# Order and budgets in a fused expert stage: where comparisons, gathers and reloads stand

## The reference

```python
q = (hb @ wq).reshape(tc, PEER_HEADS, 2, PEER_HALF)
s = jnp.einsum('thpk,hpnk->thpn', q, keys)                  # 8 heads, 2 halves, 128 keys
s_top, i_top = lax.top_k(s, PEER_TOPK)                      # 16 each
cand = s_top[:, :, 0, :, None] + s_top[:, :, 1, None, :]
cid = i_top[:, :, 0, :, None] * N_KEYS + i_top[:, :, 1, None, :]
best, pos = lax.top_k(cand.reshape(tc, PEER_HEADS, -1), PEER_TOPK)
eid = jnp.take_along_axis(cid.reshape(tc, PEER_HEADS, -1), pos, -1)
g = jax.nn.softmax(best.astype(jnp.float32), -1).astype(hb.dtype)
act = jax.nn.gelu(jnp.einsum('td,thed->the', hb, u[eid]), approximate=False)
return jnp.einsum('the,thed->td', g * act, v[eid])
```

## Time and profile before

| | us |
|---|---|
| median of 3 runs | 3791.73 (3785.59 to 3792.56) |
| the profiled execution | 3789.86 |
| its span | 3787.8 |
| granted TensorE clock over the span | 0.974 |
| busy: TensorE, weight loads, VectorE, ScalarE, GpSimd | 3556.8, 3153.1, 2732.2, 1689.3, 395.3 |
| phase U without tables, from 488.2 | 177.7 |
| phase U with tables, from 666.0 | 542.8 |
| between the phases | 23.5 |
| phase V | 558.6 |
| from V's last product to the next one | 34.0 |

### The profile page before, as it was taken

The page is one execution under the profiler, slowest core; times in us unless marked ns, Lnnn a source line. Parts: engine busy times, 40 slices in busy tenths (PEclk is TensorE's granted clock), DMA queues, the critical chain, the costliest instruction groups (busy, mean ns, idle before and its releaser), DMA issues. The chain is left out here.

```text
span 3787.8 us, 56067 instructions
## 1 busy us (share of the span) xinstructions
PE 3556.8 (94%) x21807; PEld 3153.1 (83%) x21807; DVE 2732.2 (72%) x5456; ACT 1689.3 (45%) x3029; POOL 395.3 (10%) x282
## 2 busy tenths in 40 slices
PE   7999999999997999998699999999997899989899
PEld 5777998999897877887577999998886888988798
DVE  4557366878786888888546797778887767766775
ACT  4344233555554333333434444443334535564554
POOL 0000000000454343343200000000000000000000
PEclk9999999999999999999899999999998999999999
DMA  5133366544899999998213575556665213442243
GB/s 229 63 132 133 114 244 253 186 168 167 324 352 346 332 390 365 369 381 310 85 51 145 184 231 186 167 184 229 251 242 187 112 72 146 181 169 90 83 173 139
DMA packets 181767, 773.02 MB, mean 204 GB/s; under 512 B 22976, under 2 KB 70592, under 8 KB 131584
## 3 DMA queue, kind: packets, MB, share of 16 engines
q1 hardware_dynamic: 144640, 635.20, 46.3%
q0 software_dynamic: 36864, 134.23, 9.4%
HBM read 699.38 MB, written 69.99 MB: 203 GB/s over the span
## 5 line engine op out<-in xcount | busy, mean ns | idle before, releaser
L2907 DVE TENSOR_TENSOR expert_ring_low<-expert_ring,expert_high 128x1024 fp32r<-128x1024 f32 x256 | 312.9, 1222 | 169.9 <-ACT expert_high L3236 166.6
L2192 ACT ACTIVATE expert_high<-expert_ring 128x1024 fp32r<-128x1024 f32 x256 | 270.6, 1057 | 211.3 <-PE ps L2119 211.3
L1922 DVE TENSOR_TENSOR expert_ring_low<-expert_ring,expert_high 128x1024 fp32r<-128x1024 f32 x256 | 311.7, 1219 | 70.7 <-ACT expert_high L2192 70.7
L3133 PE MATMUL ps<-hidden_high,expert_high 128*128 128x384 f32 x1024 | 353.7, 345 | 0.0
L3135 PE MATMUL ps<-hidden_high,expert_ring_low 128*128 128x384 f32 x1024 | 344.2, 336 | 0.0
L3134 PE MATMUL ps<-hidden_low,expert_high 128*128 128x384 f32 x1024 | 343.8, 336 | 0.0
L3236 ACT ACTIVATE expert_high<-expert_ring 128x1024 fp32r<-128x1024 f32 x256 | 270.0, 1055 | 118.0 <-PE ps L3170 112.5
L3424 POOL DMA_INDIRECT x<-in_peer_rows,spots x128 | 181.4, 1417 | 1107.7 <-DVE spots L2979 605.0
L2088 PE MATMUL ps<-peer_hT_high_peer,expert_high 128*128 128x256 f32 x1024 | 293.9, 287 | 0.6 <-DVE expert_ring_low L1922 0.5
L2090 PE MATMUL ps<-peer_hT_high_peer,expert_ring_low 128*128 128x256 f32 x1024 | 287.0, 280 | 0.0
L2089 PE MATMUL ps<-peer_hT_low,expert_high 128*128 128x256 f32 x1024 | 287.0, 280 | 0.0
(11 more groups left out here) (777 smaller groups left out, 9762.4 us busy)
## 6 DMA issues: line engine op xcount, KB each, us to landing
expert_ring<-in_peer_u SPq DMA_DIRECT2D x128, 1024.0 KB
expert_ring<-in_peer_v SPq DMA_DIRECT2D x128, 1024.0 KB
weight_ring<-in_ffn_w_up SPq DMA_DIRECT2D x22, 2048.0 KB, 7.5
weight_ring<-in_w_in SPq DMA_DIRECT2D x14, 2048.0 KB, 7.3
weight_ring<-in_w_mod SPq DMA_DIRECT2D x12, 2048.0 KB, 7.5
mod_slot<-in_w_mod SPq DMA_DIRECT2D x12, 2048.0 KB, 10.5
pair_weights<-pair_weights_out SPq DMA_DIRECT2D x24, 1024.0 KB
gelu_first<-gelu_out SPq DMA_DIRECT2D x62, 384.0 KB
```

The costliest lines, as they stand in the source:

```text
L1922: dve.tensor_tensor(piece(low, n), piece(raw, n), high[:, n % LEAD, :].bitcast(F32), ALU.subtract).then_inc(low_done, 1)
L2192: act.activation(high[:, n % LEAD, :], piece(raw, n), ACT.Identity).then_inc(high_done, 1)
L2907: dve.tensor_tensor(self.piece(G.e_low, n), self.piece(G.e_raw, n), G.e_high[:, n % LEAD, :].bitcast(F32), ALU.subtract).then_inc(self.S.l ...
L3133: pe.matmul(o, b[:, s], B.hs[0][:, c, 0:DW], start=(c == 0), stop=False)
```

## The change

VectorE's and ScalarE's order within a round of phase U: compares, and shares, come first. In 12 rounds (60 to 82, every second) two groups are built, so the last group stands in round 115. The budgets are new: 3900 ns in the first rounds, 3300 with tables, 2200 once the selection is done, none from round 120 on, 1450 in phase V. The last 20 gelu rows stay on the chip (16 in a new buffer, `gelu_kept`). SyncE issues the first loads of gelu rows and pair weights when round 125 has been scored; the pair weights' buffer moves to the place of the table's stage, one-hot and share buffers. The first V round takes its tiles in the order 1, 2, 0, so only the third waits for the last gelu. `x` is reloaded at round 124 of phase V.

```diff
-EARLY_NS, TABLE_NS, DOWN_NS = 2600, 2300, 1700
+EARLY_NS, TABLE_NS, PICKS_NS, DOWN_NS = 3900, 3300, 2200, 1450
+PAUSE_FROM = 120
+STAY, RING = 20, 4
+    def gelu_at(self, e):
+        return self.B.ge_out[:, e % RING, :] if e < N_KEYS - STAY + RING else self.B.ge_kept[:, e - (N_KEYS - STAY + RING), :]
+    def tables_in(self, r):
+        return [g for g in range(TABLES) if TABLE_ROUND[g] == r]
+DOUBLED = range(60, 84, 2)
+TABLE_ROUND = [r for r in range(TABLES_AT, N_KEYS) for _ in range(2 if r in DOUBLED else 1)][0:TABLES]
...
+    def up_budget(self, r):
+        if "selected" not in self.at:
+            return EARLY_NS if r < TABLES_AT - 1 else TABLE_NS
+        return PICKS_NS if r < PAUSE_FROM else 0
@@ ExpertsVector.run, phase U
+            for g in self.tables_in(r + 1):
+                self.equal(dve, g)
             if r < N_KEYS - 1:
                 self.split_low(dve, r + LEAD)
-            if 0 <= r + 1 - TABLES_AT < TABLES:
-                self.equal(dve, r + 1 - TABLES_AT)
-            left += EARLY_NS if r < TABLES_AT - 1 else TABLE_NS
+            left += self.up_budget(r)
             while left > 0:
                 left -= next(pieces, left)
@@ ExpertsTensor.products_v
-        for t in range(DT):
+        for t in (1, 2, 0):
+            if r == 0 and t == 0:
+                pe.wait_ge(S.gelu_done, N_KEYS)
@@ ExpertsScalar.run, phase U
+            if r == N_KEYS - 1:
+                self.high_weights(act, 0)
+                self.high_weights(act, 1)
+            for g in self.tables_in(r + 1):
+                self.shares(act, g)
             self.gelu(act, r)
             if r in (0, 2):
                 keep_rows(r // 2)
             self.split_high(act, r + LEAD)
-            if 0 <= r + 1 - TABLES_AT < TABLES:
-                self.shares(act, r + 1 - TABLES_AT)
...
-            if r > TABLES_AT:
-                self.table_out(act, r - TABLES_AT - 1)
+            for g in self.tables_in(r - 1):
+                self.table_out(act, g)
@@ ExpertsSync.run
+            if p == UNITS_U - 2:
+                assert stored == BLOCKS
+                sp.wait_ge(S.table_ready, DT)
+                for b in range(2):
+                    sp.wait_ge(self.ge_stored[b], 16 * (N_KEYS - STAY) // (2 * UJ))
+                self.load_ge(sp, 0)
+                self.load_ge(sp, 1)
+                for b in range(2):
+                    sp.wait_ge(self.w_stored[b], 16 * BLOCKS // 2)
+                self.load_w(sp, 0)
+                self.load_w(sp, 1)
...
             if r == N_KEYS - E_SLOTS:
+                sp.wait_ge(S.aw_done, self.weights_end(W_LOADS - 2))
+                sp.dma_start(B.x_last[:, :], G.x_spill[:, SPARSE, :]).then_inc(S.x_landed, 16)
+                sp.wait_ge(S.dotted, PAIRS)
+                sp.dma_start(G.x[:, 0:SPARSE, :], G.x_spill[:, 0:SPARSE, :]).then_inc(S.x_landed, 16)
                 G.ws.refill(sp, S.pv_done, (N_KEYS - E_SLOTS,))
         G.ws.refill(sp, S.pv_done, (N_KEYS, N_KEYS, N_KEYS))
-        sp.wait_ge(S.dotted, PAIRS)
-        sp.dma_start(G.x[:, 0:SPARSE, :], G.x_spill[:, 0:SPARSE, :]).then_inc(S.x_landed, 16)
@@ first_experts
-    B.w_in = room(96, 24).take("pair_weights_in", [P, 2, BLOCKS, 8 * BLOCK], F32)
+    B.w_in = room(16, 24).take("pair_weights_in", [P, 2, BLOCKS, 8 * BLOCK], F32)
+    B.ge_kept = room(96, 24).take("gelu_kept", [P, STAY - RING, DW], F32)
```

More of the change, by code:

```diff
@@ L2876, in expert @@
     def expert(self, r):
-        return (r + N_KEYS - KEPT) % N_KEYS
+        return (r + N_KEYS - STAY) % N_KEYS
+    def gelu_at(self, e):
+        return self.B.ge_out[:, e % RING, :] if e < N_KEYS - STAY + RING else self.B.ge_kept[:, e - (N_KEYS - STAY + RING), :]
     def scores_of(self, g):
@@ L3046, in weigh @@
         n, j = self.weights_of(r)
-        m = r // 4 - 1
-        if r < KEPT:
+        m = (r - STAY) // 4
+        if r < STAY:
             dve.wait_ge(S.gelu_done, self.expert(r) + 1)
@@ L3055, in weigh @@
             dve.wait_ge(S.aw_split, r)
-        ge = B.ge_out[:, r, :] if r < KEPT else B.ge_in[:, m % 2, r % 4, :]
+        ge = self.gelu_at(self.expert(r)) if r < STAY else B.ge_in[:, m % 2, r % 4, :]
         w = B.w_in[:, n % 2, :, j * BLOCK:(j + 1) * BLOCK]
@@ L3079, in run @@
             at["now"] = r
+            for g in self.tables_in(r + 1):
+                self.equal(dve, g)
             if r < N_KEYS - 1:
                 self.split_low(dve, r + LEAD)
-            if 0 <= r + 1 - TABLES_AT < TABLES:
-                self.equal(dve, r + 1 - TABLES_AT)
-            left += EARLY_NS if r < TABLES_AT - 1 else TABLE_NS
+            left += self.up_budget(r)
             while left > 0:
                 left -= next(pieces, left)
-        assert at["selected"] < N_KEYS - 8
+        assert at["selected"] < N_KEYS - STAY
         for r in range(2):
@@ L3213, in run @@
                     mod.sums(pe, u, S.parts_out, S.sums_ready)
-            if r >= TABLES_AT:
-                self.table_of(pe, r - TABLES_AT)
-        pe.wait_ge(S.gelu_done, N_KEYS)
+            for g in self.tables_in(r):
+                self.table_of(pe, g)
+        pe.wait_ge(S.gelu_done, N_KEYS - 1)
         pe.wait_ge(S.w_out, TABLES)
@@ L3240, in gelu @@
         act.wait_ge(S.scored, r + 1)
-        if r % 2 == 0 and p >= 2:
+        if r % 2 == 0 and 2 <= p < (N_KEYS - STAY + RING) // 2:
             act.wait_ge(self.ge_stored[p % 2], 16 * (p // 2))
-        act.activation(self.B.ge_out[:, r % 4, :], self.G.ps[:, r % 3, 0:DW], ACT.Gelu).then_inc(S.gelu_done, 1)
+        act.activation(self.gelu_at(r), self.G.ps[:, r % 3, 0:DW], ACT.Gelu).then_inc(S.gelu_done, 1)
     def shares(self, act, g):
@@ L3306, in run @@
                     mod.out(act, S.sums_ready, S.mod_out)
-            if r > TABLES_AT:
-                self.table_out(act, r - TABLES_AT - 1)
+            for g in self.tables_in(r - 1):
+                self.table_out(act, g)
             self.gates(act, r)
-        self.table_out(act, TABLES - 1)
-        for r in range(3):
-            self.high_weights(act, r)
+        self.high_weights(act, 2)
         for r in range(N_KEYS):
@@ L3337, in load_ge @@
         if m >= 2:
-            sp.wait_ge(self.S.aw_done, KEPT + 4 * (m - 1))
+            sp.wait_ge(self.S.aw_done, STAY + 4 * (m - 1))
         sp.dma_start(B.ge_in[:, m % 2, :, :], B.ge_dram[:, 4 * m:4 * m + 4, :]).then_inc(self.ge_landed[m % 2], 16)
@@ L3344, in load_w @@
             sp.wait_ge(self.S.aw_done, self.weights_end(n - 2))
-        first = (N_KEYS - KEPT, 0)[n > 0] if n == 0 else 8 * n - 8
+        first = self.expert(0 if n == 0 else self.weights_end(n - 1))
         size = 8 if 0 < n < W_LOADS - 1 else KEPT
@@ L3358, in run @@
             self.load_unit(sp, p + E_SLOTS)
-            if UJ * p < N_KEYS - KEPT:
+            if UJ * p < N_KEYS - STAY:
                 sp.wait_ge(S.gelu_done, UJ * (p + 1))
@@ L3367, in run @@
                     mod.load(sp, u + 2, self.mod_landed)
-            while stored < BLOCKS and TABLES_AT + 4 * stored + 5 <= UJ * p + 1:
+            while stored < BLOCKS and TABLE_ROUND[4 * stored + 3] + 2 <= UJ * p + 1:
                 self.store_w(sp, stored)
                 stored += 1
[L3371 to L3381, removed]
+            if p == UNITS_U - 2:
[9 more added lines that the diff above has]
+                self.load_w(sp, 1)
         for q in range(UNITS_U):
@@ L3386, in run @@
                 self.load_unit(sp, UNITS_U + q + E_SLOTS)
-            if q % 2 == 1 and 2 <= q // 2 + 1 < (N_KEYS - KEPT) // 4:
-                self.load_ge(sp, q // 2 + 1)
+            if r % 4 == 0 and 2 <= (r - STAY) // 4 + 1 < (N_KEYS - STAY) // 4:
+                self.load_ge(sp, (r - STAY) // 4 + 1)
             n = (r - KEPT) // 8 + 2
@@ L3394, in run @@
                 sp.dma_start(B.rows_b[:, :], B.ln_b.partition_broadcast(P)).then_inc(S.rows_landed, 16)
-                sp.dma_start(B.x_last[:, :], G.x_spill[:, SPARSE, :]).then_inc(S.x_landed, 16)
                 sp.dma_start(G.front.q.raw[:, :, :], G.front.q.src).then_inc(S.q_landed, 16)
             if r == N_KEYS - E_SLOTS:
+                sp.wait_ge(S.aw_done, self.weights_end(W_LOADS - 2))
+                sp.dma_start(B.x_last[:, :], G.x_spill[:, SPARSE, :]).then_inc(S.x_landed, 16)
+                sp.wait_ge(S.dotted, PAIRS)
+                sp.dma_start(G.x[:, 0:SPARSE, :], G.x_spill[:, 0:SPARSE, :]).then_inc(S.x_landed, 16)
                 G.ws.refill(sp, S.pv_done, (N_KEYS - E_SLOTS,))
         G.ws.refill(sp, S.pv_done, (N_KEYS, N_KEYS, N_KEYS))
-        sp.wait_ge(S.dotted, PAIRS)
-        sp.dma_start(G.x[:, 0:SPARSE, :], G.x_spill[:, 0:SPARSE, :]).then_inc(S.x_landed, 16)
         sp.wait_ge(S.rows_landed, 32)
```

## The result

The changed kernel takes 3877.5 us (median of four runs, 3875.7 to 3884.9) against 3789.9: the ratio of the means is 1.0236, 95% interval 1.0218 to 1.0254. 3881 was forecast. The profiled execution has a span of 3873.9 us, 86.1 more than before.

What follows compares the result with a forecast made beforehand. A ring through ScalarE and VectorE (5.51 us a round) was taken to bound table rounds, with the pieces joining it after the change. +144.1 - 17.5 - 22 - 14.7 = +89.9 us on 3789.9 gave 3881 on the median; range 3842 to 3928.

Steps and rivals of the forecast that it cites:

- The ring: Phase U table rounds: new order puts VectorE's pieces inside the two-engine ring, 5.03 us plus pieces; phase U +144 us; chance 0.83.
- The early rounds: Phase U before the tables: VectorE gets 1.3 us more per round, still covered; 3 us added (0 to 10).
- the signs: Table rounds in the profile after: shares wait 2 to 3.5 us for the compare, VectorE about 2.7 for the high part.
- The hole: Between phases U and V: earlier loads and 20 kept gelu rows leave 6 us of hole, -17.5 us.
- Phase V: Phase V: fewer gathers and gelu loads take the transfer engines out of saturation, -22 us (bounds 0 and 30).
- gelu waits as many as before: Phase V: VectorE's waits for gelu rows, 58.3 us in 18 places before; an unchanged count would show the forecast wrong.
- The end: After V: x reload issued at round 124 of V, 16 us earlier, spares the next stage's wait, -14.7 us (10 to 17).
- The second: Phase U: new order breaks the ring and TensorE sets the round at 5.07 us; 3683 us on the median; chance 0.07.
- The third (the clock): Table rounds: TensorE's clock falls to 1.2 GHz in most, rounds of 7.5 us against 7.1, about 3922 us; chance 0.09.
- my argument that gaps of 2 us are too short for a fall: TensorE in table rounds: 2 us gaps are shorter than any the rows show followed by a clock fall; against third rival.

Runs made afterwards that it cites:

- the two half-width runs: Dots and sums of gathered rows over 512 of 1024 columns, on the changed kernel (3826.1 us) and on the kernel before (3786.6 us).
- more traffic: Changed kernel plus 32 transfers of 512 KB in phase V into a buffer nobody reads: 3905.9 us, V 565.1 us.
- the kernel with only half of the order edit: Changed kernel with only ScalarE's order undone (gelu, high part, then shares), VectorE keeping compares first: 3697.5 us, ratio 0.9769 to the kernel before.

## Why the prediction was right, step by step

**The ring.** Forecast 5.03 us plus the pieces, measured 6.18 with one piece of 1.14 and 7.37 with two. The first 21 rounds after round 32 average 8.46 us (8.3 forecast). Four rounds with two doubled ones (66 to 69) take 11.67 + 6.71 + 7.24 + 5.07 = 30.7 us (4 x 7.1 + 2 x 1.18 = 30.8). The rounds from 117 on take 4.16 us (4.25 forecast). Phase U ended at 1349.6; 1352.9 was forecast: +140.9 us for +144.1. The early rounds cost 0.5 us where I had put 3. That the pieces lie in the ring after and not before is shown from both sides by the two half-width runs: 57.0 us against 4.1.

**Where I misread the signs.** I expected ScalarE's shares to wait 2 to 3.5 us a round; it is 341.2 / 84 = 4.1, because ScalarE is done with the eviction 0.8 us before the low part ends and then waits through the pieces and the compare. VectorE's 247.0 / 94 = 2.6 us was as forecast (2.7).

**The hole.** -17.0 us for -17.5. The early issue is worth 8.3 of them; the prediction had not told it from the tables' earlier end and the rest. SyncE's queue in the kernel after (timeline, against the earlier trace rows):

```profile
1342.10 0.84 SPq L3359 DMA_DIRECT2D gelu_in<-gelu_first  x2
1343.03 8.50 SPq L3367 DMA_DIRECT2D pair_weights_in<-pair_weights  x2
```

**Phase V.** -19.8 us for -22. I had named "gelu waits as many as before" as a sign that this step was wrong. They are as many:

```profile
DVE weighted L3070 <- DMA gelu_in<-gelu_first: 54.2, 17, 6.5
```

The step held all the same: what fell is the part of them that reached TensorE, whose idle time went from 19.7 to 8.5 us. That is 11 of the 20 us; the other 9 are TensorE's busy time, 538.9 us at a granted clock of 0.98 before and 530.1 at 1.00 after. The count of a wait on an engine off the critical path was a poor sign. Nor do the kept rows give the time by themselves: in the first 20 rounds, which need no reloaded gelu row now, V gained 1.5 us (85.0 to 83.5), and 18.3 in the 108 rounds after them. That traffic is the cause is supported by more traffic bringing the time back and by lighter pieces not taking it away; it isn't shown, since the added transfers lengthened SyncE's list too.

**The end.** -15.3 us for -14.7; undoing this step alone gave it back.

**The sum** of the stages is +0.5 + 140.4 - 17.0 - 19.8 - 15.3 = +88.8 us (89.9 forecast), and the rest of the span, where the work is the same, is 2.7 us shorter. The single terms were off by up to 3 us, in both directions, so that the sum is closer than its parts is in part luck. The range on record, 3842 to 3928, is also a little wider than the -35 and +45 that it is said to follow from.

**The rivals.** The second (order broken, TensorE sets the round, 3683) did not come about, but its number is close to that of the kernel with only half of the order edit: 3697. The third (the clock): it does fall. In 24 of the rounds from 34 to 116 the products run at the lower level for a part of the round. Ten of these rounds lie in the selection, up to round 53, behind idle stretches of 3.1 to 4.8 us; the others follow stretches of 1.7 to 2.5 us, as here (timeline, TensorE, kernel after):

```profile
1126.75 1.27 PE L3175 MATMUL ps<-hot_weighted,equal 128*128 128x128 f32 x8 [1.91 <-ACT hot_weighted L3269]
...
1128.04 0.52 PE L3151 MATMUL ps<-hidden_low,expert_high 128*128 128x384 f32 x1
```

The same product takes 0.33 us at 2.4 GHz. So my argument that gaps of 2 us are too short for a fall was wrong; the granted clock is 0.91 over the tables. What makes it harmless is the ring. Such a round of products lasts 5.6 us or a little more instead of 4.1. In 14 of the 23 with a group it still ends before the shares of that group are done, in the others up to 3.4 us after. The shares of the next round come 7.37 us later all the same, as in the rounds at full clock with two pieces, and over the table rounds the list of waits has none of ScalarE or VectorE for TensorE. The one exception is round 116, which has no table and whose pace TensorE sets: part of it ran at the lower level, and it took 5.84 us instead of 4.16.

The Trainium skill (TensorE: Matmul & The Clock Gate, "HAM oscillation — how this bites in real kernels") tells of a kernel whose bursts of products start cold after every wait, and which pays for it each time. The trace agrees in part: the falls are there, but in 24 rounds and not in all, and in the rounds with tables they were not paid, because TensorE wasn't what the others waited for.

## What to carry to other kernels

When two engines hand work to each other every round, write down the ring: the steps from an instruction to its own successor through both program orders, with their durations from the trace. If the sum is the period, everything in the ring costs its full length, and an edit that moves an instruction "ahead" may pull work into it that used to lie beside it. Here it paid to move the producer (the compare) forward and to leave the consumer (the shares) where it was. Try the halves of such a pair of moves one by one, where the program's orders allow each.

## What the runs showed of the hardware that I had not expected

Idle stretches of one length had both outcomes for TensorE's clock. Of the 16 stretches of 1.90 to 1.94 us in front of a group from round 87 on, five were followed by products at the 1.2 GHz level and eleven were not, and the one of 3.12 us in the earlier trace rows was followed by none. Issuing two loads of pair weights, of 0.75 and 1.5 MB in rows of 256 and 512 bytes, held SyncE's queue for 7.0 us in the kernel before and 8.5 in the changed one (5.8 to 10.7 over all runs), and the load of `v` behind them was issued right after that, at 1351.6.
